# Two of seven projection tiles of the mixing layers in split rounded products instead of plain float32 products

## The reference, cut to what matters

```python
for l in range(DEPTH):                      # DEPTH = 2
    x = layer_norm(ALPHA * x + swiglu_half(x, ffn1_w1[l], ffn1_w3[l], ffn1_w2[l]), ln1_g[l], ln1_b[l])
    h = x @ w_in[l]                         # (256 x 1024) @ (1024 x 3360)
    (a_u, a_v, b_qkv, b_z, b_beta, b_decay, c_q, c_k, c_v, c_r, c_g) = jnp.split(h, split_at, axis=-1)
    ...                                     # three small mixers: gating, gated delta rule, gated linear attention
    mix = jnp.concatenate([out_a, out_b, out_c], axis=-1) @ w_out[l]
```

## Time and profile before

| | |
|---|---|
| median of 3 runs | 2262.51 us (2259.31 to 2262.86) |
| the profiled execution, its own time | 2261.65 us |
| its span in the profile | 2259.9 us |
| TensorE busy | 2192.0 us (97%), 12161 records |
| TensorE weight loads busy | 1322.1 us (59%) |
| VectorE, ScalarE, GpSimd busy | 964.9 us (43%), 679.6 us (30%), 92.4 us (4%) |
| HBM traffic | 279 GB/s over the span |

### The profile page before, as it was taken

The page is one execution under the profiler, slowest core; times in us unless marked ns, Lnnn a source line. Parts: engine busy times, 40 slices in busy tenths (PEclk is TensorE's granted clock), DMA queues, the critical chain, the costliest instruction groups (busy, mean ns, idle before and its releaser), DMA issues. The chain is left out here.

```text
span 2259.9 us, 29771 instructions
## 1 busy us (share of the span) xinstructions
PE 2192.0 (97%) x12161; PEld 1322.1 (59%) x12162; DVE 964.9 (43%) x1387; ACT 679.6 (30%) x1095; POOL 92.4 (4%) x139
## 2 busy tenths in 40 slices
PE   8999999999999999999999999999999999999998
PEld 7887776788788867768887753333333333333332
DVE  4563684666575438547549752221111111112111
ACT  4432332544343323244335641111111111111111
POOL 5000020000000001100002000000000000000000
PEclk9999999999999999999999999999999999999999
DMA  8763421776387442148744579999999999999998
GB/s 296 245 233 99 148 77 39 242 261 226 109 284 262 164 143 75 40 131 282 267 177 139 197 286 424 428 428 429 427 429 429 427 428 429 429 427 428 429 429 351
DMA packets 192725, 632.36 MB, mean 280 GB/s; under 512 B 31281, under 2 KB 127553, under 8 KB 166257
## 3 DMA queue, kind: packets, MB, share of 16 engines
q1 hardware_dynamic: 192624, 630.93, 72.4%
HBM read 629.82 MB, written 1.07 MB: 279 GB/s over the span
## 5 line engine op out<-in xcount | busy, mean ns | idle before, releaser
L410 PE MATMUL banks<-ffn_room 128*128 128x512 f32 x1920 | 453.7, 392 | 0.0
L410 PEld LDWEIGHTS banks<-ffn_room 128*128 128x128 f32 x1920 | 357.5, 188 | 72.8
L527 DVE TENSOR_TENSOR ffn_room<-memory,ffn_room 128x2048 fp32r<-128x2048 f32 x124 | 281.0, 2292 | 99.5 <-ACT ffn_room L487 99.4
L3064 DVE TENSOR_SCALAR attend_words<-banks 128x512 f32<-128x512 f32 x32 | 22.1, 691 | 564.0 <-PE banks L2800 564.0
L487 ACT CAST ffn_room<-memory 128x2048 fp32r<-128x2048 f32 x124 | 232.2, 1903 | 70.7 <-PE banks L428 62.8
L428 PE MATMUL banks<-ffn_room 128*128 128x512 f32 x1056 | 248.1, 390 | 0.3
L2800 PE MATMUL banks<-memory 128*64 128x512 f32 x1088 | 243.9, 596 | 0.0
L428 PEld LDWEIGHTS banks<-ffn_room 128*128 128x128 f32 x1056 | 197.6, 188 | 42.7 <-DVE ffn_room L566 2.1
L2800 PEld LDWEIGHTS banks<-memory 128*64 128x64 f32 x1088 | 75.4, 136 | 151.9 <-issue 150.1
L2800 PE MATMUL banks<-attend_later,memory 128*64 128x512 f32 x672 | 152.0, 594 | 0.1
L493 ACT ACTIVATE memory<-banks 128x256 f32<-128x256 f32 x88 | 33.8, 385 | 341.7 <-PE banks L410 318.9
(11 more groups left out here) (440 smaller groups left out, 2463.9 us busy)
## 6 DMA issues: line engine op xcount, KB each, us to landing
memory<-in_ffn_w SPq DMA_DIRECT2D x132, 1024.0 KB, 7.4
memory<-in_w_gate_up SPq DMA_DIRECT2D x62, 2048.0 KB, 22.3
attend_later<-in_w_gate_up SPq DMA_DIRECT2D x39, 2048.0 KB, 23.8
memory<-in_w_down SPq DMA_DIRECT2D x25, 2048.0 KB, 24.2
attend_later<-in_w_down SPq DMA_DIRECT2D x19, 2048.0 KB, 23.2
attend_words<-in_w_gate_up SPq DMA_DIRECT2D x17, 2048.0 KB, 22.3
memory<-in_w_in SPq DMA_DIRECT2D x32, 1024.0 KB, 6.2
memory<-in_w_ada SPq DMA_DIRECT2D x32, 768.0 KB, 5.1
```

The lines of the kernel that those rows point to most:

```text
L410: m = nc.tensor.matmul(psum[:, GU + tt, :], x_parts[:, xp, k, tt * P:tt * P + P], rows, start=(n == 0), stop=(n == 3 * KD - 1))
L527: tt_op(b, chip.ring[:, chip.slot(base + i), :], a.bitcast(F32), ALU.subtract).then_inc(chip.used, 1)
L3064: ts(room.gate, psum[:, GATE_BANK, :], 7.0, None, ALU.min).then_inc(s["g_ready"], 1)
```

## The change

`IN_PARTS = (1, 2)` names the tiles that are computed in parts: tile 1 (the second half of the small columns) and tile 2 (the q columns of the delta rule). The k tile is tile 3 and stays as it was, as do tiles 0, 4, 5 and 6. For the two tiles and for x, ScalarE writes the rounded part into free room (`lead`), VectorE the remainder (`low`); the remainder of a weight tile overwrites the tile in its ring slot. Units 2 to 5 then run `unit_in_parts` in place of `unit`.

```diff
+IN_PARTS = (1, 2)
...
+    by_k = lambda v: v.rearrange("p (k t) -> p k t", k=KD)
+    x_parts = (by_k(free[:, 0:2048]), by_k(x_low))
+    lead_rooms = (chip.tmp_rounded, free[:, 2048:4096], late[:, 0:2048], late[:, 2048:4096])
+
+    def tile_parts(t, i):
+
+        cols = WIN_TILES[t][2]
+        slot = chip.slot(base + 2 * t + i)
+        return (lead_rooms[2 * (t - IN_PARTS[0]) + i][:, 0:4 * cols], chip.ring_low[:, slot, 0:4 * cols],
+                chip.ring[:, slot, 0:4 * cols])
...
+            def unit_in_parts(n, t, half, kind, cols):
+
+                pe.wait_ge(s["low"], 2 * (t - IN_PARTS[0]) + 3)
+                pe.wait_ge(s["evac"], n - 1)
+                parts = [[tile_parts(t, i)[p].rearrange("p (k n) -> p k n", k=4) for i in range(2)] for p in range(2)]
+                for c in range(2 if kind == "channels" else 1):
+                    cc = (2 * half + c) * P
+                    for k in range(KD):
+                        for xp, wp in PASSES:
+                            x, rows = x_parts[xp][:, k, :], parts[wp][k // 4][:, k % 4, :]
+                            first, last = k == 0 and (xp, wp) == PASSES[0], k == KD - 1 and (xp, wp) == PASSES[2]
+                            if kind == "channels":
+                                m = mm(psum[:, n % 2, c * 256:c * 256 + 256], rows[:, cc:cc + P], x, start=first, stop=last)
+                            else:
+                                m = mm(psum[:, n % 2, 0:cols], x[:, half * P:half * P + P], rows, start=first, stop=last)
+                m.then_inc(*((s["unit"], 1) if half == 0 else (chip.used, 2)))
...
-            for n in range(4):
+            def lead(t, i):
+                chip.arrived(act, base + 2 * t + i)
+                part, _, whole = tile_parts(t, i)
+                copy(part, whole).then_inc(s["lead"], 1)
+
+            copy(x_parts[0], chip.xT).then_inc(s["lead"], 1)
+            lead(1, 0)
+            lead(1, 1)
+            evac(0)
+            lead(2, 0)
+            lead(2, 1)
+            for n in range(1, 4):
                 evac(n)
...
             take_mod(chip, s)
+            dve.wait_ge(s["lead"], 1)
+            tt_op(x_parts[1], chip.xT, x_parts[0].bitcast(F32), ALU.subtract).then_inc(s["low"], 1)
+            for n, (tile, i) in enumerate((tile, i) for tile in IN_PARTS for i in range(2)):
+                dve.wait_ge(s["lead"], n + 2)
+                part, rest, whole = tile_parts(tile, i)
+                tt_op(rest, whole, part.bitcast(F32), ALU.subtract).then_inc(s["low"], 1)
             finish_x(chip, s, dve, chain)
```

More of the change, by code:

```diff
@@ L115, in __init__ @@
         self.mod_rows = self.norm_gb[0:3, 1, 512:1024]
+        self.tmp_rounded = self.rounded[:, w.at:w.at + self.NT * D]
         self.tmp = w.take(self.NT * D).rearrange("p (t d) -> p t d", t=self.NT)
+        self.ring_low = self.rounded[:, w.at:w.at + RING * SLOT].rearrange("p (s n) -> p s n", s=RING)
         self.ring = w.take(RING * SLOT).rearrange("p (s n) -> p s n", s=RING)
@@ L717 @@
        "ub_mm wt_mm ub wt scan_a scan_q u_rows scan_o o_rows scan_s state b_ss b_rms b_out "
-       "early_turned early_T b_turned b_T mixed ") + POST_NORM
+       "early_turned early_T b_turned b_T mixed lead low ") + POST_NORM
 def mix_loads(chip, l, w_in, w_out):
@@ L730, in head_of, with mix_phase @@
     return 2 * (e % 4) + e // 4
-def mix_phase(chip, s, spent, l, loads, base, par, gamma_beta, skip, room, rows_before, mod_before):
+def mix_phase(chip, s, spent, l, loads, base, par, gamma_beta, skip, room, rounded, rows_before, mod_before):
     nc, D, KD, NT = chip.nc, chip.D, chip.KD, chip.NT
@@ L749, in mix_phase @@
     LT, PT = (per_head(region[:, 1024 * i:1024 * i + 1024]) for i in range(2))
+    x_low = rounded("low", w.at + 1024, 2048)
     region2 = w.take(3072)
@@ L752, in mix_phase @@
     bqT = region2[:, 0:2048].rearrange("p (t g k n) -> p t g k n", t=NT, g=4, k=2)
+    free = rounded("free", w.at, 4096)
     qkv = take3(NT, 3 * B_W)
@@ L756, in mix_phase @@
     dm = per_head(dm)
+    late = rounded("late", w.at + 1024, 4096)
     early = w.take(2048)
@@ L860, in unit @@
                 kind, c0, cols = WIN_TILES[t]
+                if t in IN_PARTS:
+                    unit_in_parts(n, t, half, kind, cols)
+                    return
                 if k0 == 0:
@@ L3271 @@
 FFN_STEP = 256
-WIDE_SET, SLIM_SET = 100, 32
+WIDE_SET, SLIM_SET = 102, 32
 START = "chain ident x c turned"
@@ L3317, in build, with rounded @@
         ffn(0, masks if l == 0 else None)
+        at = -(-nc.sbuf_base // 32) * 32
         with nc.sbuf_tensor(f"mix_room_{l}", [P, chip.words - chip.fixed], F32) as room:
-            mix_phase(chip, sm, sf.span(), l, loads, base[3 * l + 1], mix_par, (a["ln2_g"], a["ln2_b"], l), alpha, room,
+            def rounded(name, word, words):
+                odd = word % 8
+                return nc.alloc_sbuf_tensor_at(f"mix_{name}_{l}", [P, words + odd], F32R, offset=at + 4 * (word - odd))[:, odd:odd + words]
+            mix_phase(chip, sm, sf.span(), l, loads, base[3 * l + 1], mix_par, (a["ln2_g"], a["ln2_b"], l), alpha, room, rounded,
                       (a["ln1_g"], a["ln1_b"], l), mod_row[0:1, 2 * l * ADA_BLOCK:(2 * l + 1) * ADA_BLOCK])
```

## The result

| | before | changed kernel |
|---|---|---|
| median of the runs measured side by side | 2261.99 us (4 runs) | 2247.98 us (4 runs, 2246.62 to 2251.76) |
| ratio | | 0.9944, 95% interval 0.9931 to 0.9957 |
| the profiled execution, its own time | 2261.65 us | 2248.24 us |
| its span | 2259.9 us | 2246.6 us |

The changed kernel is faster by 14.0 us; 8.9 were forecast, and 2247.98 lies under the range of 2249.5 to 2260.5. The direction was right and the size wrong. The two profiled executions differ by 13.4 us, and that is the difference to be found in the traces.

What follows compares the result with a forecast made beforehand. TensorE was taken to bound the mixing phases, with the end set by the expert weight stream moving along. Units 2 to 5 save 4.46 us a layer, 8.9 in two: 2262.5 - 8.9 = 2253.6 us, range 2249.5 to 2260.5.

Steps and rivals of the forecast that it cites:

- What bounds, and that the saving travels: TensorE bounds the mixing phases; the chain behind unit 5 moves by the full 4.46 us, the expert weight stream along.
- the 0.47 us at L935: Behind unit 5: TensorE was said to wait 0.47 us for GpSimd's L839 and L935.
- Price of a rounded product: Units 2 to 5: one pass plus 13.7 ns, 0.1804 us for 400 columns, 0.1204 for 256; two layers save 8.9 us.
- the bounds of 6.3 and 11.9: Two-layer saving in us if rounded products pay 23 ns beyond their columns (6.3) or only 3.5 ns (11.9).
- cheap short products: Rival, units 2 to 5: short rounded products cost no more than plain ones beyond their columns; 2250.6 us, chance 0.14.
- the page's quarter: Units 2 to 5: three passes for four would save a quarter, 12.4 us in two layers, giving 2250.1 us.
- Weight load not hidden: Rival, units 2 to 5: loads don't hide behind 256 columns, 0.214 us a product; slower at 2271.5 us, chance 0.08.
- ScalarE and VectorE: Mixing phases: five added casts and five subtractions a layer end in time, covered by idle time, and cost nothing.
- the ten passes: The added casts on ScalarE and subtractions on VectorE, put at 19.6 us a layer, all covered by idle time.
- Profiled execution 2261.65 - 8.9: Whole kernel: the units' saving of 8.9 us taken off the profiled execution, giving 2252.8 us.
- Half-clock stretch ahead of the experts: Ahead of the experts the clock stood at half for 7 us; it may shift, 1 to 3 us either way.
- The range: Whole kernel: 2249.5 to 2260.5 us, taking in both bounds, the scatter and a saving caught in part.

Runs made afterwards that it cites:

- e3: Kernel before the change with 25 tiny 8x8 products added at TensorE's start, in its wait for x: 2262.55 us, 1.0011 of the kernel before.
- e2: Only tile 2 (q) computed in parts, tile 1 plain as in the kernel before: 2257.24 us, 0.9990 of the kernel before.
- e6: Changed kernel with 42 tiny 8x8 products added at TensorE's start, in its wait for x: 2255.26 us, 0.9974 of the kernel before.
- e5: Changed kernel run again with no edit, on a second chip: 2248.80 us, 0.9937 of the kernel before.
- e11: Changed kernel run once more with no edit, on a third chip: 2249.75 us, 0.9958 of the kernel before.
- e1: Only tile 1 computed in parts, q plain as in the kernel before: 2258.53 us, 0.9994 of the kernel before.
- e7: Changed kernel with the k tile (tile 3, units 6 and 7) in parts too: 2248.99 us, 0.9944 of the kernel before.

## Why the prediction was right or wrong

- **What bounds, and that the saving travels.** Right. The table of places shows no wait that took a part of it back; GpSimd's L839 (now L856) starts at 250.49 instead of 254.91, 4.42 us earlier. The stream of the experts' weights moved along. One row was misread: the 0.47 us at L935 are idle time of the weight loads alone, TensorE's products there had no wait.
- **Price of a rounded product.** Right. Over unit 2 and 3 a product of 400 columns takes (230.68 - 221.56) / 48 = 0.190 us with the last one's tail in it, 0.183 between neighbours (forecast 0.180); of 256 columns about 0.12 (forecast 0.120). The units saved 9.2 us against 8.9, well between the bounds of 6.3 and 11.9. Two small errors cancel in part: units 2 and 3 saved 2.0 us a layer for 2.14, units 4 and 5 saved 2.6 for 2.32. Neither cheap short products nor the page's quarter (12.4 us) came, though the time of 2250.1 that the quarter gave looks nearer to the measured 2247.98 than mine. That is chance: whoever read the total alone would have taken the wrong price for the right one.
- **Weight load not hidden.** Wrong by its rows: 0.12 us between products with a load each. The rule of the Trainium skill ("TensorE: Matmul & The Clock Gate", Part 3, What overlaps and what doesn't) would make it at least 0.21 us here, an estimate from 0.107 for the load and 0.107 for the pass; the trace disagrees.
- **ScalarE and VectorE.** Right. The cast of 1600 columns took 1.52 us for 1.61, the subtraction 1.82 for 1.83; the margins were 1.09 us for the first copy (forecast 0.6) and 3.0 for unit 2 (forecast 2.9). L1323 (now L1377) waits 0.62 us, forecast 1.2: `finish_x` started 0.9 us later than before. (By their own terms the ten passes sum to 19.5 us a layer, not 19.6; nothing rests on it.)
- **The step that failed** is the sentence that makes the whole out of the phases: "Profiled execution 2261.65 - 8.9". It takes all behind unit 5 as rigid and puts what the longer stream does there at nothing, without a reason. The change adds 48 records a layer to TensorE's stream, and stops that stand at every 128th record fall on other products of the 64x64 runs, where they meet the load of `w_out` at another moment. In the pair of profiled executions that gave 71.90 - 69.96 = 1.9 us; over all profiles of the two kernels, 72.0 - 70.7 = 1.3 us. The row was there to be read: L1001, 1.80 us of "issue" after 214 products; the order of the instructions gave the 48.
- **Half-clock stretch ahead of the experts.** The text put 1 to 3 us either way in the range, and 1.6 came, in our favour. Over the profiles of unchanged code its length was 6.8 us and none (before), 3.4, 13.7 and none (changed kernel), so this part of the 13.4 us belongs to the execution, not to the change.
- **Sum.** 9.2 (units) + 1.9 (the two runs) + 1.6 (clock ahead of the experts) = 12.7 of 13.4 us; the other 0.7 comes behind 1390 us, in steps of both signs (-0.5, +1.5 and -0.4 us). The three measurements of the changed kernel, 0.9944, 0.9937 and 0.9958, average 0.9946, which is 12.2 us; the last one's interval holds the forecast's ratio, 2253.6 / 2262.5 = 0.9961. Against that average 9.2 us is shown to come from the units and about 1.3 from the stops (from two and three profiles, whose sums differ by up to 1.3 us among themselves); the 1.7 left are open. Clock stretches behind the mixing are the likeliest source, but no run isolates them.
- **The range** was too narrow at its low end: its bounds came from the price of the products and the clock, and no term stood for the stops.

## What to carry to other kernels

Before you cost an edit, look for idle time called "issue" in runs of short instructions, and count at which instruction it stands. If the edit adds or removes instructions ahead of it, that stop moves and can change by 2 us, more if the clock falls behind it; a result within a few microseconds then says little about the edit. Test it with filling that is hidden in a wait: a whole period must give the same time, another part of one shows what the place is worth. Look at the very end of the kernel too, where the same filling cost 2.6 us. And look at which transfers run beside the stop. And when half of an edit is worth nothing and the whole more than forecast, don't average: look at what both moved.

## What the runs showed of the hardware

- **Stops at every 128th record of TensorE.** Each record is a weight load and a product, two instructions. In the 64x64 runs, where a product starts every 0.030 us ((7.87 - 0.22) / 253), the stops are 127 products apart in a row such as e3's; outside the products of 64x64 TensorE shows no "issue" idle over 0.3 us in a place. The page lists instruction transfers by themselves, before and after:

```profile
q8 instruction: 75, 1.23, 0.2%
```

```profile
q8 instruction: 76, 1.25, 0.2%
```

  That is 16.4 KB each. The Trainium skill ("Runtime: NRT & Kernel Launch", Instruction fetch mechanics) says that instructions come in blocks of 16 KiB, 256 of them, and that crossing into the next costs little and is mostly hidden. 128 records of two instructions agree with the 256, and outside these runs, but for the last branch of e2 and e6, the traces agree with "hidden". Here it isn't: 0.2 to 2.8 us, each time ended 1.2 to 1.6 us after a block on q8 had landed.
- **Its size depends on where it falls beside a load.** After 161 to 166 products 0.15 to 1.2 us, after 182 1.5, after 193 to 225 1.8 to 2.8, after 247 to 260 1.2 to 1.8, after 288 to 292 0.2 to 0.8. The boundary 128 products ahead is crossed 1.9 to 2.9 us into the run for the longest, 0.8 to 1.8 us after the load of `w_out` began, and the next block then starts 3.3 to 4.3 us behind it. Crossed 1.0 to 1.2 us into the run the block starts 1.8 to 2.7 us behind, at 3.6 to 3.9 us 2.8 to 3.2 us, at 4.8 us 2.0 to 2.1 us. Two executions of one kernel can part here: in layer 1 the changed kernel crosses a boundary 0.1 us ahead of the load. In its first profile the block started 0.2 us later and the stop after 161 products was spared, in e5 and e11 it started 2.6 to 2.7 us later and the stop was 1.18 and 1.02 us. How queues share the transfer engines isn't shown.
- **A block can also be missing at the end.** In e6 and e2 the profile is 2.6 and 2.1 us longer behind the last product than in the 11 others, with TensorE in its last branch.
- **The clock falls behind the longest stops.** It went to half for 3.4 us in the run behind stops of 1.91 to 2.83 us (e1 twice, e6 twice, e3 and e7 in layer 1), but not behind e2's of 2.26 nor behind any of the shorter ones. Some 70 products in 3.4 us instead of 110 cost about 1.2 us each time.
